# Near term of the state-space layer as a block Toeplitz product, and the next head's scores placed ahead of the value products

## Time and profile before

| | |
|---|---|
| median of 3 runs | 1561.54 us (1561.12 to 1563.14) |
| the profiled execution's own time | 1561.48 us |
| its span, first to last instruction | 1559.7 us |
| mean granted clock of TensorE | 0.989 |
| PE busy over the span | 1423.8 us (91%) |
| DVE busy | 568.9 us (36%) |
| ACT busy | 318.1 us (20%) |
| POOL busy | 128.0 us (8%) |
| HBM read | 455.66 MB, 296 GB/s over the span |

### The profile page before, as it was taken

One profiled execution on the slowest core, in us unless ns is written; L12 is line 12 of the kernel. 1 busy time (PEld: TensorE's weight loads), 2 busy tenths in 40 slices (PEclk: granted clock), 3 DMA queues, 4 the chain that ended last, 5 costly groups with the idle time before them and its releaser, 6 DMA issues.

```text
span 1559.7 us, 17091 instructions
## 1 busy us (share of the span) xinstructions
PE 1423.8 (91%) x6847; PEld 784.9 (50%) x6847; DVE 568.9 (36%) x1005; ACT 318.1 (20%) x497; POOL 128.0 (8%) x187
## 2 busy tenths in 40 slices
PE   7999699999898898898898898998799999999997
PEld 6778333443332332332332332332489777778875
DVE  6785502120120120120120120120587576656663
ACT  6582100000000000000000000000432433324321
POOL 1030000000000000000000000000223033331001
PEclk9999899999999999999999999999899999999998
DMA  9034599999999999999999999999362212215231
GB/s 325 1 120 204 216 395 428 428 428 425 429 428 429 427 429 429 428 428 428 429 427 429 429 429 427 428 429 429 137 213 92 72 44 68 68 36 208 81 109 54
DMA packets 66317, 462.60 MB, mean 297 GB/s; under 512 B 5216, under 2 KB 32096, under 8 KB 41568
## 3 DMA queue, kind: packets, MB, share of 16 engines
q1 hardware_dynamic: 62576, 454.71, 70.6%
q0 software_dynamic: 3408, 6.82, 1.5%
q10 hardware_dynamic: 288, 0.45, 0.1%
HBM read 455.66 MB, written 6.29 MB: 296 GB/s over the span
## 4 chain that ended last, share of the span: by engine, by line
PE 58%; DMA 33%; DVE 4%; ACT 3%; issue 1%; POOL 0%; POOLq 0%; ACTq 0%; DVEq 0%
DMA wide<-in_w_down 23%; PE bank L773 14%; DMA early<-in_w_down 10%; PE bank L568 8%; PE bank L569 8%; PE bank L570 8%; PE bank L800 6%; PE bank L813 4%; PE bank L918 1%; PE bank L855 1%; PE bank L876 1%; PE bank L737 1%; PE bank L553 1%; PE bank L744 1%; ACT pT L986 1%
## 5 line engine op out<-in xcount | busy, mean ns | idle before, releaser
L773 PE MATMUL bank<-wide,xinT 128*64 128x512 f32 x1376 | 306.9, 596 | 47.7 <-DMA wide<-in_w_up 26.8
L773 PEld LDWEIGHTS bank<-wide,xinT 128*64 128x64 f32 x1376 | 95.6, 137 | 257.2 <-issue 171.9
L1394 DVE SCALAR_TENSOR_TENSOR th<-th,bank 128x512 f32<-128x512 f32 x32 | 20.6, 684 | 432.4 <-ACT th L1137 432.4
L773 PE MATMUL bank<-early,xinT 128*64 128x512 f32 x672 | 150.5, 596 | 25.7 <-DMA early<-in_w_up 14.7
L800 PE MATMUL bank<-wide,actT 128*64 128x512 f32 x688 | 153.0, 595 | 3.7 <-issue 3.0
L568 PE MATMUL bank<-hT_lo,ring_r 128*128 128x512 f32 x352 | 140.3, 399 | 0.0
L570 PE MATMUL bank<-hT_hi,ring_r 128*128 128x512 f32 x352 | 137.1, 390 | 0.0
L569 PE MATMUL bank<-hT_hi,ring_r 128*128 128x512 f32 x352 | 137.0, 389 | 0.0
L1137 ACT ACTIVATE th<-bank 128x512 f32<-128x512 f32 x32 | 17.4, 594 | 515.7 <-PE bank L773 515.7
L773 PEld LDWEIGHTS bank<-early,xinT 128*64 128x64 f32 x672 | 46.0, 137 | 129.3 <-issue 79.1
L1391 DVE TENSOR_TENSOR ring_r<-ring,ring_r 128x2048 fp32r<-128x2048 f32 x38 | 88.6, 2331 | 46.8 <-ACT ring_r L1002 46.7
(11 more groups left out here) (329 smaller groups left out, 1721.2 us busy)
## 6 DMA issues: line engine op xcount, KB each, us to landing
wide<-in_w_gate SPq DMA_DIRECT2D x43, 2048.0 KB, 40.1
wide<-in_w_up SPq DMA_DIRECT2D x43, 2048.0 KB, 39.1
wide<-in_w_down SPq DMA_DIRECT2D x43, 2048.0 KB, 38.4
early<-in_w_gate SPq DMA_DIRECT2D x21, 2048.0 KB, 40.1
early<-in_w_up SPq DMA_DIRECT2D x21, 2048.0 KB, 39.2
early<-in_w_down SPq DMA_DIRECT2D x21, 2048.0 KB, 38.5
ring<-in_w_in SPq DMA_DIRECT2D x26, 1024.0 KB, 5.1
ring<-in_w_out SPq DMA_DIRECT2D x8, 1024.0 KB, 5.0
```

Source lines behind the costliest of these rows:

```text
L773: last = pe.matmul(bank[1 + 2 * (m % 2) + q // 2][o:o + 64, :], xinT[:, k, :], w[:, i, q * 512:(q + 1) * 512], start=(k == 0), stop=(k == ...
L1394: return dve.scalar_tensor_tensor(out_, a, s, b, op0, op1)
```

## The change

- The near term is computed per group of 16 channels. DVE writes the lag products into `lagsb` (seven blocks of zeros, then lags 0 to 7, the skip added to lag 0). POOL writes them to a DRAM scratch, waits, and gathers eight shifted copies into `toep`, one 128 by 128 matrix per group. `ssm_out` waits for them (`toep_in`) and issues, between the two far-term matmuls of a pair of groups, two matmuls of 64 columns with `toep` as weights and `ubuf` as input, accumulated in the same bank. The nine near matmuls, ACT's copy and DVE's addition are gone.
- `ubuf` holds all four chunks, in the place of `uT`, and is gathered once by eight DMAs four times as large, ahead of `output_table(0)`. The rows of `ubuf` are in reverse order of time, as is the input table.
- `head_values` is split: the transposes of head i, then the scores of head i+1, then the value products of head i. Head 0's scores stay at the start. DVE's order of softmax, states and input table is as before.
- The router's tiles are computed in two pairs after all transposes, the tiles of a pair alternating matmul by matmul in different strips of 32 output rows.
- At the end ACT squares half tiles, POOL adds the two sums, DVE mixes the multiplications by the gain for tiles 0 and 1 with the additions, and tiles are multiplied and stored in halves.
- DVE's preamble of the second block has one more memset and one small reduction.

```diff
@@ -357,9 +360,9 @@
         for i in range(STEPS):
-            if i < HEADS:
+            if i == 0:
                 for q in range(TT):
-                    jobs.add(f"score{i}_{q}")
+                    jobs.add(f"score0_{q}")
             for n in range(2):
...
@@ -367,6 +370,9 @@
                     jobs.add(f"probT{i}_{b}")
+                if i + 1 < HEADS:
+                    for q in range(TT):
+                        jobs.add(f"score{i + 1}_{q}")
                 jobs.add(f"pv{i}")
...
@@ -526,10 +531,11 @@
-            for t in range(TT):
-                sp.wait_ge(final_ready, t + 1)
-                sp.dma_start(out[t * P:(t + 1) * P, :], xres[:, t, :]).then_inc(stored, 16)
-            sp.wait_ge(stored, 16 * TT)
+            for o in range(2 * TT):
+                t, h = o // 2, slice(o % 2 * 512, o % 2 * 512 + 512)
+                sp.wait_ge(final_ready, o + 1)
+                sp.dma_start(out[t * P:(t + 1) * P, h], xres[:, t, h]).then_inc(stored, 16)
+            sp.wait_ge(stored, 16 * 2 * TT)
...
@@ -614,16 +620,18 @@
-            def routed(t):
+            def routed(tiles):
                 wr = col("w_router", 0, KT * 2 * NE).rearrange("p (k e) -> p k e", k=KT)
-                for h in range(2):
-                    was_read(pe, f"xb{t}_{h}")
-                b = start("logitT") if t == 0 else bank[jobs.bank("logitT")]
+                for t in tiles:
+                    for h in range(2):
+                        was_read(pe, f"xb{t}_{h}")
+                b = start("logitT") if tiles[0] == 0 else bank[jobs.bank("logitT")]
                 for k in range(KT):
-                    last = pe.matmul(b[32 * t:32 * t + 32, 0:P], wr[:, k, :], xT[k // 4][:, k % 4, t * P:(t + 1) * P],
-                                     start=(k == 0), stop=(k == KT - 1))
-                if t == TT - 1:
+                    for t in tiles:
+                        last = pe.matmul(b[32 * t:32 * t + 32, 0:P], wr[:, k, :], xT[k // 4][:, k % 4, t * P:(t + 1) * P],
+                                         start=(k == 0), stop=(k == KT - 1))
+                if tiles[-1] == TT - 1:
...
@@ -645,8 +653,6 @@
                             turned(o // 2 - 1)
-                            if o > 3:
-                                routed(o // 2 - 2)
...
@@ -708,8 +714,8 @@
             turned(TT - 1)
-            routed(TT - 2)
-            routed(TT - 1)
+            routed((0, 1))
+            routed((2, 3))
...
@@ -855,7 +861,7 @@
-            def head_values(h):
+            def head_probs(h):
...
@@ -866,6 +872,8 @@
                     finish(f"probT{h}_{piece}", last)
+
+            def head_values(h):
                 r = 64 * (h % 2)
...
@@ -907,32 +915,27 @@
                         at = ri * 256 + (g // 2) * NCH
-                        last = pe.matmul(b[r:r + 64, at:at + NCH], st[:, ri, g // 2, r:r + 64], ubuf[:, g, :],
+                        last = pe.matmul(b[r:r + 64, at:at + NCH], st[:, ri, g // 2, r:r + 64], ubuf[:, c, g, :],
...
-                was_read(pe, f"lags_{c}")
-                b = start(f"near{c}")
-                for lag in range(T8 + 1):
-                    n = (T8 - lag % T8) * NCH
-                    last = pe.matmul(b[:, S - n:S], kbd[:, lag, :],
-                                     uT[:, c, :, :].rearrange("p t j -> p (t j)")[:, 0:n],
-                                     start=(lag == 0), stop=(lag == T8))
-                finish(f"near{c}", last)
-
...
                 pe.wait_ge(states_ready, c + 1)
+                pe.wait_ge(toep_in, 16 * T8 * (c + 1))
...
                 for g in range(CGP):
-                    for ri in range(2):
-                        last = pe.matmul(b[:, g * P:(g + 1) * P], wc[:, ri, g, SG:SG + P],
-                                         hbd[:, ri, g, :, :].rearrange("p a b -> p (a b)"),
-                                         start=(ri == 0), stop=(ri == 1))
+                    far = [(wc[:, ri, g, SG:SG + P], hbd[:, ri, g, :, :].rearrange("p a b -> p (a b)"))
+                           for ri in range(2)]
+                    pe.matmul(b[:, g * P:(g + 1) * P], *far[0], start=True, stop=False)
+                    for n in (2 * g, 2 * g + 1):
+                        pe.matmul(b[:, n * NCH:(n + 1) * NCH], toep[:, n, :], ubuf[:, c, n, :],
+                                  start=False, stop=False)
+                    last = pe.matmul(b[:, g * P:(g + 1) * P], *far[1], start=False, stop=True)
...
             for i in range(STEPS):
-                if i < HEADS:
-                    head_scores(i)
+                if i == 0:
+                    head_scores(0)
...
@@ -940,6 +943,9 @@
                 if i < HEADS:
+                    head_probs(i)
+                    if i + 1 < HEADS:
+                        head_scores(i + 1)
...
@@ -1225,8 +1231,6 @@
                     copy_out(f"ssm{c}", flat(ybuf))
-                if i % 2 == 1 and i < 2 * CT:
-                    copy_out(f"near{i // 2}", uT[:, i // 2, :, :].rearrange("p t j -> p (t j)"))
...
@@ -1260,10 +1264,11 @@
                 weights_hi(M + u)
-            for t in range(TT):
-                was_read(act_e, f"fin{2 * t + 1}")
-                act_e.activation(nrm[:, t, :], xres[:, t, :], ACT.Square,
-                                 accum_out=stat[:, 48 + t:49 + t]).then_inc(square_sum, 1)
+            for o in range(2 * TT):
+                was_read(act_e, f"fin{o}")
+                h = slice(o % 2 * 512, o % 2 * 512 + 512)
+                act_e.activation(nrm[:, o // 2, h], xres[:, o // 2, h], ACT.Square, scale=D ** -0.5,
+                                 accum_out=stat[:, 40 + o:41 + o]).then_inc(square_sum, 1)
...
@@ -1321,11 +1326,9 @@
-            def inputs(c):
-
-                for t in range(T8):
-                    pool.dma_start(ubuf[t * SG:(t + 1) * SG, :, :],
-                                   u_dram[c * P:(c + 1) * P, t, :].rearrange("(g c) j -> c g j", c=SG)).then_inc(u_in, 16)
+            for t in range(T8):
+                pool.dma_start(ubuf[(T8 - 1 - t) * SG:(T8 - t) * SG, :, :, :].rearrange("h c g j -> h (c g) j"),
+                               u_dram[:, t, :].rearrange("(q h) j -> h q j", h=SG)).then_inc(u_in, 16)
...
@@ -1356,13 +1359,18 @@
-            inputs(0)
...
             for c in range(CT):
+                was_read(pool, f"lags_{c}")
+                pool.dma_start(l_dram[c], lagsb.rearrange("p d c -> p (d c)")).then_inc(l_out, 16)
+                pool.wait_ge(l_out, 16 * (c + 1))
+                row = (2 * T8 - 1) * SG
+                for t in range(T8):
+                    pool.dma_start(toep[t * SG:(t + 1) * SG, :, :],
+                                   bass.AP(tensor=l_dram.tensor, offset=c * P * row + t * SG,
+                                           ap=[[row, SG], [SG * row, CG], [1, P]])).then_inc(toep_in, 16)
                 if c + 1 < CT:
-                    full(pool, f"state{c}")
-                    inputs(c + 1)
...
@@ -1375,7 +1383,13 @@
             pool.dma_start(gfin, gfin_d.partition_broadcast(P)).then_inc(gfin_in, 16)
-            roots(48, 2 * TT)
+            for t in range(TT):
+                c = stat[:, 48 + t:49 + t]
+                pool.wait_ge(square_sum, 2 * TT + 2 * t + 1)
+                link(pool.tensor_scalar(c, stat[:, 40 + 2 * t:41 + 2 * t], 1.0, EPS, ALU.mult, ALU.add))
+                pool.wait_ge(square_sum, 2 * TT + 2 * t + 2)
+                link(pool.tensor_tensor(c, c, stat[:, 41 + 2 * t:42 + 2 * t], ALU.add))
+                pool.tensor_tensor(stat[:, 52 + t:53 + t], c, stat[:, 62:63], ALU.pow).then_inc(root_mean, 1)
...
@@ -1865,12 +1881,10 @@
                     if c:
-                        full(dve, f"near{c - 1}")
-                    dve.tensor_scalar(kbd[:, T8, :], ident, col("skip", c), None, ALU.mult)
-                    read(name, tt(kbd[:, 0:T8, :].rearrange("p d (g c) -> p d g c", g=CG),
-                                  bank[jobs.bank(name)][:, 0:P].rearrange("p (d c) -> p d c", d=T8).unsqueeze(2)
-                                  .to_broadcast([P, T8, CG, SG]),
-                                  group_of.unsqueeze(1).unsqueeze(3).to_broadcast([P, T8, CG, SG]), ALU.mult))
+                        dve.wait_ge(l_out, 16 * c)
+                    b = bank[jobs.bank(name)]
+                    stt(lagsb[:, T8 - 1, :], diag, col("skip", c), b[:, 0:SG], ALU.mult, ALU.add)
+                    read(name, dve.tensor_copy(lagsb[:, T8:, :].rearrange("p d c -> p (d c)"), b[:, SG:P]))
...
@@ -1880,10 +1894,8 @@
                     for c in cs:
-                        y, near, s = yT[:, c, :], uT[:, c, :, :].rearrange("p t j -> p (t j)"), tmp[:, c % 2, :]
+                        y, s = yT[:, c, :], tmp[:, c % 2, :]
                         dve.wait_ge(y_in, 16)
-                        was_read(dve, f"near{c}")
-                        link(tt(y, y, near, ALU.add))
...
@@ -1939,11 +1951,25 @@
             dve.wait_ge(x_back, 16)
-            residual("fin", 0.5)
```

(42 more changed lines are left out.)

## The result

The changed kernel takes 1569.51 us (median of 5 runs, 1568.62 to 1571.59), against 1561.54 (5 runs, 1561.12 to 1563.14): a ratio of 1.0048, 95% interval 1.0037 to 1.0058. It is 8.0 us slower. The forecast was 0.8 slower, in a range that ended half a microsecond lower, at 1569. The profiled execution took 1570.14 us with a span of 1568.1, so 8.7 and 8.4 us over the one of before; mean granted clock 0.977 instead of 0.989.

What follows compares the result with a forecast made beforehand. PE was taken as the bound while the heads run. Terms -20.2 + 7.4 - 6.6 + 18.7 + 7.2 - 3.3 - 2.4 = +0.8 gave 1562.3 us, range 1554 to 1569.

Steps and rivals of the forecast that it cites:

- Near term and Toeplitz products: On PE, four chunks: near matmuls removed, -20.2 us; Toeplitz matmuls added at 1.85 per chunk, +7.4 us.
- Copies' waits: PE's waits for ACT's copies of the probabilities vanish for seven heads, with scores between transposes and values: -6.6 us.
- The stall: PE waits 6.2 us for DVE's softmax in steps 2, 4 and 6: +18.7 us.
- The clock: PE's clock falls in each of the three stalls and costs 2.4 us each time: +7.2 us.
- The rival: Low clock stays through PE's sparse work after each stall: +30, 1592; half run low, 1570; chance 0.15 above 1566.
- the third rival: Transposes don't count for PE's clock, so recovery starts after them: 1.1 us more lost per stall, 1565.6; chance 0.07.
- Router: Router calls on PE run as two pairs in alternating strips, passing on through the experts: -3.3 us.
- The end: Final squares, multiplications and stores in halves, the last store 0.6 us less: -2.4 us, bounds -1 and -3.5.
- Nothing else was late: POOL and DMA work costed at nothing; closest is `output_table` before the next lags, with 0.6 us of cover.

Runs made afterwards that it cites:

- Experiment 3: The changed kernel with six extra 512-column matmuls on PE ahead of the wait for the probabilities of heads 2, 4 and 6: 1558.71 us.
- experiment 4: The changed kernel with six extra 512-column matmuls on PE behind the wait for the probabilities, ahead of the transposes of heads 2, 4 and 6: 1579.38 us.
- experiment 5: The changed kernel with the scores back at the start of their step and the Toeplitz form kept: 1566.11 us.
- experiment 2: The changed kernel with only DVE's input table moved from before the next head's softmax to behind the gates of that step: 1556.40 us.
- experiment 1: The changed kernel with DVE's order turned in even steps: softmax first, then states, low part of the weights, gates and input table: 1541.61 us.
- experiment 8: The kernel of experiment 1 with the gates' products ahead of `weights_lo` on DVE in step 2: 1537.78 us.
- experiment 6: The kernel before with only the scores moved ahead of the value products, the near term staying nine matmuls: 1559.89 us.

## Why the prediction was wrong

**Near term and Toeplitz products** were right: -20.2, and 4 x 1.78 = +7.1 instead of +7.4. The weights do set the pace.

**Copies' waits**: right, 7.5 to 0.9, -6.6.

**The stall**: right in place, number and size, 3 x 6.16 = +18.5 instead of +18.7. DVE's chain takes 17.2 us, and PE had only 11 us of gates to run beside it.

**The clock** is the step that failed. The prediction was right that PEclk falls in each stall, and took "4 to 5.4 us at half speed" after each from the earlier trace rows. It was 9.8 to 10.2. By the rows above, step 2 lost 1.08 in the transposes, 2.21 in the scores and 1.41 in the values, 4.7; steps 4 and 6, whose values take 3.85 and 3.93 us to the next row, lost 4.8 and 4.9. That is **+14.4** instead of +7.2, and a pair of steps took 51 us instead of about 49. The rival had it in its middle case: "If half of them are run low, 5 lost each, 1570", at a chance of 0.15 for anything above 1566. Against it I had held that the clock came back while only transposes ran. But those were 32 in a row, and here ten are followed by scores with 64 rows of weights and values with 64 columns of weights. Experiment 3 shows that without the idling there is no such cost. In experiment 4 the clock came back sooner with other work behind the same wait (three of three steps), but in experiment 5 it did so with transposes and values alone behind a shorter one. So what follows the wait counts, as experiment 4 has it, but dense work is not the only thing that brings the clock back sooner. Which product holds the clock down, and why 2.17 us of idling brought low stretches of 6.8 to 10.2 us in experiment 2 and one of 3.4 in experiment 1, stays open. So the third rival (transposes don't count) was not tried by itself either.

The Trainium skill, TensorE: Matmul & The Clock Gate, Part 1, says that for modeling the slow start is below 1% of a typical span and that the number of slow matmuls varies from run to run of one kernel. The traces agree with both: the 14.4 us are 0.9% of 1568.1, and of two profiled executions of the kernel of experiment 8, one has a low stretch of 3.4 us near 113 us and the other has none. Yet 14.4 us is more than the whole difference between the two kernels.

**Router**: right. The logits' copy to `logT` starts at 163.31 instead of 166.76, -3.4, and the first transposes of the second block at 1111.54 instead of 1114.93.

**The end**: the chain became what was forecast, from ACT's last square (0.63 us) to the last multiplication, ended 4.1 us after the last addition's start instead of 6.0. The last store landed 0.6 us sooner after its issue, as costed, but 1.3 us came on between its landing and the end of the span (4.0 instead of 2.7), which the sum had not: -1.2 instead of -2.4.

**Nothing else was late**, as costed. POOL's `output_table` and `toep` made nobody wait; the table ends at 1290.40 and the next lags start at 1290.80. The cover forecast there, 0.6 us, is 0.4.

The sum with measured terms: -20.2 + 7.1 - 6.6 + 18.5 + 14.4 - 3.4 - 1.2 = +8.6, against 8.7 between the profiled executions and 8.0 between the medians. Of the 7.8 us that the forecast of +0.8 lacked, the clock has 7.2 and the end 1.2; the Toeplitz term gave 0.3 back, the stall 0.2 and the router 0.1.

## What to carry to other kernels

Work taken from the engine that is the bound may have been the cover of another engine's chain: write down, for each wait on it, what now stands between the start of that chain and the wait, and if it is shorter than the chain, reorder the other engine in the same change. Here moving the softmax ahead of the states on DVE turned +8 into -21 us, and one bank wait more, moved, into -25. Two moves that use the same cover can't be costed apart. A wait on TensorE can cost more than its length (6.2 us cost 4.8 more here, 2.2 us between 1.7 and 5.0 more, and 1.1 us between gates nothing): price the slow stretch by the work that follows the wait in this place, and not by a stretch elsewhere that has other work.

## What the runs showed that was not expected

- A wait of 2.17 us was enough for 1.2 GHz afterwards (experiments 1 and 2, four waits of four), in three of them only 0.5 to 1.1 us after PE had resumed. Waits of 1.1 us in experiment 6 were followed by none, but they have 512-column products around them. The waits for the copies in the kernel before, 0.9 to 1.0 us among the sparse products, were followed by none either.
- After the same 6.15 us wait the clock was back in 2.9 to 6.1 us with 512-column products, and in 9.8 to 10.2 with transposes, scores and values. After a wait of 3.8 us, with transposes and values only, it was back in 5.9 to 8.9.
- Matmuls with 128 by 128 weights cost 0.11 to 0.12 us a record whether they have 64 or 128 columns: 1.78 us for 16 and 1.89 us for 16.
- The tail behind the last DVE operation is 6.0 us with the Toeplitz part and 5.2 to 5.3 without, with four stores or eight: half the bytes land 0.6 us sooner, and the end comes 0.4 to 0.6 later behind them.
